# Six of sixteen weight tiles of a modulation gate move from TensorE to VectorE, and their partial sums are added in a later block

## The reference, cut to what matters

```python
def modulate(x, norm_g, ada):
    shift, scale, gate = jnp.split(ada, 3, axis=-1)
    return rmsnorm(x, norm_g) * (1 + scale) + shift, gate

def mixer_layer(x, xc, c_act, cc_act, norm_g, w_ada, b_ada, w_in, ...):
    h, gate = modulate(x, norm_g, (c_act @ w_ada + b_ada)[:, None, :])
    hc, gate_c = modulate(xc, norm_g, cc_act @ w_ada + b_ada)
    u = h @ w_in
    ...                      # convolution, recurrence, windowed attention, each with its own gate path
    x = x + gate * (jnp.concatenate([y_conv, y_lru, y_attn], axis=-1) @ w_out)
    ...
    xc = xc + gate_c * (jnp.concatenate([yc_conv, yc_lru, yc_attn], axis=-1) @ w_out)
```

## Time and profile before

| | us |
|---|---|
| median of 3 runs | 1241.3 |
| lowest, highest | 1240.75, 1241.37 |
| the profiled execution, its time | 1241.5 |
| the profiled execution, span from the first to the last instruction | 1239.7 |
| TensorE busy in the span | 1198.3 |
| VectorE busy | 852.1 |
| ScalarE busy | 555.6 |

### The profile page before, as it was taken

The page is one execution under the profiler, slowest core; times in us unless marked ns, Lnnn a source line. Parts: engine busy times, 40 slices in busy tenths (PEclk is TensorE's granted clock), DMA queues, the critical chain, the costliest instruction groups (busy, mean ns, idle before and its releaser), DMA issues.

```text
span 1239.7 us, 16341 instructions
## 1 busy us (share of the span) xinstructions
PE 1198.3 (97%) x6518; PEld 958.5 (77%) x6518; DVE 852.1 (69%) x1291; ACT 555.6 (45%) x873; POOL 10.2 (1%) x13
## 2 busy tenths in 40 slices
PE   2899999999999999999999999999999999999996
PEld 1556777767778788886888887988978988899885
DVE  5444546767656677663768998695899977657664
ACT  5222446662224434454442222454865455575542
POOL 0000100000000000000000001000000000000000
PEclk9999999999999999999999999999999999999998
DMA  9999856556753442221538887444432634325552
GB/s 335 350 348 348 257 200 250 204 204 241 277 215 133 144 162 84 69 68 68 197 122 350 324 329 261 128 140 135 138 106 77 222 136 149 122 100 202 189 171 68
DMA packets 80892, 236.32 MB, mean 191 GB/s; under 512 B 9392, under 2 KB 54192, under 8 KB 59440
## 3 DMA queue, kind: packets, MB, share of 16 engines
q1 hardware_dynamic: 80816, 235.27, 53.9%
HBM read 230.54 MB, written 2.10 MB: 188 GB/s over the span
## 4 chain that ended last, share of the span: by engine, by line
PE 88%; SPq 4%; DMA 4%; DVE 2%; ACT 2%; issue 0%; DVEq 0%; ACTq 0%
PE psum_block L837 20%; PE psum_block L838 20%; PE psum_block L839 20%; PE psum_block L834 5%; SPq L609 3%; PE psum_ada L663 3%; PE psum_block L835 2%; DMA raw<-in_w_ada 2%; PE psum_scores L919 1%; PE psum_scores L906 1%; PE psum_scores L939 1%; PE psum_scores L869 1%; PE psum_ada L710 1%; DMA bd<-in_w_ada 1%; DMA glu<-in_w_ada 1%; PE psum_misc L966 1%
## 5 line engine op out<-in xcount | busy, mean ns | idle before, releaser
L837 PE MATMUL psum_block<-h_parts,w_hi 128*128 128x512 f32 (+1 forms) x1408 | 494.3, 351 | 0.3 <-DVE h_parts L1413 0.3
L838 PE MATMUL psum_block<-h_parts,w_hi 128*128 128x512 f32 (+1 forms) x1408 | 485.3, 345 | 0.0
L839 PE MATMUL psum_block<-h_parts,w_lo 128*128 128x512 f32 (+1 forms) x1408 | 485.3, 345 | 0.0
L1421 DVE TENSOR_TENSOR w_lo<-raw,w_hi 128x1024 fp32r<-128x1024 f32 x210 | 254.6, 1223 | 257.8 <-ACT w_hi L1061 257.7
L1061 ACT ACTIVATE w_hi<-raw 128x1024 fp32r<-128x1024 f32 x210 | 220.1, 1056 | 413.5 <-PE psum_block L839 354.4
L837 PEld LDWEIGHTS psum_block<-h_parts,w_hi 128*128 128x128 f32 x1408 | 266.6, 189 | 51.5 <-issue 16.8
L838 PEld LDWEIGHTS psum_block<-h_parts,w_hi 128*128 128x128 f32 x1408 | 266.8, 189 | 33.5 <-issue 2.6
L839 PEld LDWEIGHTS psum_block<-h_parts,w_lo 128*128 128x128 f32 x1408 | 266.7, 189 | 32.4
L1706 DVE SCALAR_TENSOR_TENSOR Y<-glu,small,Y 128x512 f32<-128x512 f32 (+1 forms) x240 | 130.4, 612 | 0.0
L834 PE MATMUL psum_block<-h_parts,w_hi 128*128 128x512 f32 x240 | 84.8, 399 | 0.0
L835 PE MATMUL psum_block<-h_parts,w_lo 128*128 128x256 f32 x240 | 67.4, 281 | 0.0
(11 more groups left out here) (228 smaller groups left out, 1349.1 us busy)
## 6 DMA issues: line engine op xcount, KB each, us to landing
raw<-in_w_blocks SPq DMA_DIRECT2D x105, 1024.0 KB, 4.9
raw<-in_w_ada SPq DMA_DIRECT2D x71, 1024.0 KB, 7.0
glu<-in_w_ada SPq DMA_DIRECT2D x10, 1024.0 KB, 9.9
bd<-in_w_ada SPq DMA_DIRECT2D x10, 1024.0 KB, 9.5
qreg<-in_w_blocks SPq DMA_DIRECT2D x8, 896.0 KB, 11.6
kv<-in_w_ada SPq DMA_DIRECT2D x5, 1024.0 KB, 11.9
Y<-in_xT SPq DMA_DIRECT2D x8, 512.0 KB, 7.8
T<-in_xT SPq DMA_DIRECT2D x16, 256.0 KB, 7.0
```

What stands on the lines that cost most here:

```text
L837: mm(ps[:, cols], hi, hh[:, k, t], start=(at == 0), stop=False)
L838: mm(ps[:, cols], hi, hl[:, k, t], start=False, stop=False)
L839: last = mm(ps[:, cols], lo, hh[:, k, t], start=False, stop=(at == DT - 1))
L1421: V.tensor_tensor(wl[:, u % 4, 0:n], raw_of(item)[:, cols], wh[:, u % 4, 0:n].bitcast(F32), ALU.subtract).then_inc(*C.up("lo", u))
```

## The change

A third way is added for layer 0's gate tiles 10 to 15. VectorE multiplies each with the two conditioning vectors and adds it into running sums, `gate0_acc`: four instructions of 1024 columns per tile (two vectors, two halves), tile 10 with a plain multiplication, the others with multiply and add. The running sums lie in rows 8 to 15 of Y (left 256 columns), in rows 2 and 3, and in the second half of `bd`. Tiles 10 to 14 are loaded one after the other into rows 0, 1, 6 and 7 of Y, a single buffer outside the ring; tile 15 goes through the ring. Block 15 ends with two gate tiles on TensorE and the sum, `gate0_sum`, which is `scale_sum` with other operands. Tiles 0 to 9 move to blocks 9, 11, 12, 13 and 15; layer 1's shift tiles to blocks 16 to 23, one block later each. ScalarE waits for the sum before it splits keys and values (block 18) and before it writes attention gate 0 into Y (block 20).

```diff
+GATE0_ON_DVE = {7: [10, 11], 8: [12], 10: [13], 11: [14], 14: [15]}
+GATE0_LOADS = {8: [11], 9: [12], 10: [13], 12: [14], 14: [15]}
+GATE0_IN_Y = (10, 11, 12, 13, 14)
+GATE0_ON_PE = {9: [0, 1], 11: [2, 3], 12: [4, 5], 13: [6, 7], 15: [8, 9]}
+GATE0_SUM = 15
...
-    s += [("w", b) for b in (OPEN[0], OPEN[0] + 1)]
+    s += [("w", b) for b in (OPEN[0], OPEN[0] + 1)] + [("gate0", GATE0_IN_Y[0])]
...
             if l == 0:
-                s += [("ada", *a) for a in plan.get(b, []) if b != SCALE_SUM] + [("gate", k) for k in gates.get(b, [])]
+                s += [("gate0", k) for k in GATE0_LOADS.get(b, [])]
+                s += [("ada", *a) for a in plan.get(b, []) if a[2] != DT - 1 or a[:2] not in SUMMED]
+                s += [("gate", k) for k in gates.get(b, [])]
...
+            if SLOT[i] == Y_SLOT:
+                return Y[:, 0:12, :].rearrange("p (a b) t -> p a b t", b=6)[:, :, 0:2, :]
...
+            def gate0_sum():
+                pe.wait_ge(*C.at("pick_set"))
+                pe.wait_ge(*C.at("gate0_acc", DT - 1, 3))
+                for i in range(2):
+                    for j in range(4):
+                        part = (Y[:, 8 + 2 * j:10 + 2 * j, 0:LAT] if i == 0 else Y[:, 2 + j, :] if j < 2
+                                else bd[:, 1, 4 * (j - 2):4 * (j - 1), :])
+                        last = mm(psA[32 * j:32 * j + 32, :], pick[:, 32 - i:64 - i], part,
+                                  start=False, stop=(i == 1), tile_position=(0, 32 * j))
+                last.then_inc(*C.up("ada_mm", 0, GATE, DT - 1))
...
+                for n, (i, acc, x) in enumerate(parts_of):
+                    c = cstat[:, c_at(k) + i:c_at(k) + i + 1]
+                    if first:
+                        V.tensor_scalar(acc, x, c, None, ALU.mult).then_inc(*C.up("gate0_acc", k, n))
+                    else:
+                        dve.wait_ge(*C.ago("gate0_acc", 3))
+                        stt(acc, x, c, acc, ALU.mult, ALU.add).then_inc(*C.up("gate0_acc", k, n))
...
+                if gb == OPEN[0]:
+                    gate0_acc(GATE0_ON_DVE[b][0])
...
                 if l == 0:
+                    for k in GATE0_ON_DVE.get(b, [])[1 if b == OPEN[0] else 0:]:
+                        gate0_acc(k)
                     for k in SCALE_ON_DVE.get(b, []):
                         scale_acc(k)
```

More of the change, by code:

```diff
@@ L127, in ada_plan @@
     on_dve = sum(len(tiles) for tiles in SCALE_ON_DVE.values())
[L128 to L132, removed]
+    rest = [(1, SHIFT, k) for k in range(DT)] + [(1, SCL, k) for k in range(DT - on_dve)]
+    plan = {b: [(0, GATE, k) for k in tiles] for b, tiles in GATE0_ON_PE.items()}
+    plan[GATE0_SUM] += [(0, GATE, DT - 1)]
+    first = GATE0_SUM + 1 + DT // 2
+    for b in range(GATE0_SUM + 1, GATE1_AT):
+        if rest and (b < first or (b - first) % 2 == 0):
+            plan[b] = [rest.pop(0) for _ in range(2)]
     assert not rest
@@ L1042, in _ @@
                     misc.append(("pw_out", l, CT - 1))
[L1043 to L1046, removed]
+                for a in PLAN.get(b, []) if l == 0 else []:
+                    if a == (0, GATE, DT - 1):
+                        gate0_sum()
+                    elif a == (1, SCL, DT - 1):
+                        scale_sum()
+                    else:
                         ada_mm(*a)
@@ L1455, in gate_acc, with gate0_acc @@
                     stt(acc, w, cstat[:, c_at(k):c_at(k) + 1], acc, ALU.mult, ALU.add).then_inc(*C.up("gate_acc", k))
+            def gate0_acc(k):
+                w = raw_of(("gate0", k))
+                dve.wait_ge(*arrived(("gate0", k)))
+                halves = ([w[:, a, :, :] for a in range(2)] if k in GATE0_IN_Y else
+                          [w[:, a * 2 * TOK:(a + 1) * 2 * TOK].rearrange("p (m t) -> p m t", t=TOK) for a in range(2)])
+                quarters = [x.rearrange("p m (s t) -> p m s t", t=LAT) for x in halves]
+                latent = Y[:, 8:16, 0:LAT].rearrange("p (a m s) t -> p a m s t", a=2, s=2)
+                parts_of = ((0, latent[:, 0, :, :, :], quarters[0]), (0, latent[:, 1, :, :, :], quarters[1]),
+                            (1, Y[:, 2:4, :], halves[0]),
+                            (1, bd[:, 1, :, :].rearrange("p (m n) c -> p m (n c)", m=2), halves[1]))
+                first = k == min(min(tiles) for tiles in GATE0_ON_DVE.values())
+                if first:
+                    dve.wait_ge(*C.at("h_lo", 0, DT - 1, 1))
+                    dve.wait_ge(*used(last_of(BD_SLOT)))
+                for n, (i, acc, x) in enumerate(parts_of):
+                    c = cstat[:, c_at(k) + i:c_at(k) + i + 1]
+                    if first:
+                        V.tensor_scalar(acc, x, c, None, ALU.mult).then_inc(*C.up("gate0_acc", k, n))
+                    else:
+                        dve.wait_ge(*C.ago("gate0_acc", 3))
+                        stt(acc, x, c, acc, ALU.mult, ALU.add).then_inc(*C.up("gate0_acc", k, n))
             def scale_acc(k):
```

18 lines of the change are left out of this document (16 added, 2 removed).

## The result

The changed kernel takes 1244.06 us (median of 13 runs, 1242.19 to 1245.64), the kernel before in the same comparison 1241.41 us (1240.55 to 1241.91): 2.65 us more, a ratio of 1.0021 with a 95% interval of 1.0012 to 1.0029. The profiled execution took 1243.05 us, with a span of 1241.3 us against 1239.7 us. Lines of the code have moved: L663 is now L687, L1421 is L1462, L609 is L633, L1486 is L1550.

A forecast was written before the change was run, and what follows sets the result against it. TensorE was taken to bound the kernel: -3.7 us of work, +3.9 for waits on tiles 6 and 7, +1.9 for tile 9, about +2.0 us in all. Forecast 1243.3 us, range 1238.3 to 1246.0 us.

The forecast's parts named there:

- TensorE's ledger: Six tiles leave TensorE (5.55 us), block 15's sum adds 1.85 us: net -3.7 us if TensorE never waits.
- VectorE's ledger: Tiles 11 to 15 each add four 1024-column instructions on VectorE, 4.8 us a tile, bounds 4.4 to 5.3 us.
- Blocks 7 to 10 covered: Tiles 10 to 12 fit VectorE's idle gaps there; tile 13 in block 10 costs only 0.7 us.
- The new wait of 4.5 us in block 11: VectorE waits 4.5 us for tile 14, whose load stands behind block 14's weights; the tile ends at 230.2 us.
- The waits in block 13: TensorE waits 2.3 us for the load of gate tile 6 and 1.6 us for tile 7.
- Tile 9: In block 15 TensorE waits 1.9 us for this tile's load, which needs tile 15's buffer and lands at 274.9 us.
- Blocks 16 and 23: TensorE's wait for VectorE's gate values, +1.1 us, returns in block 16; block 23 gains a pair of 1.85 us.
- The clock: Rival, chance 0.16: a block 15 wait halves TensorE's clock, costing 1.6 us (1244.9 us); a block 13 fall costs nothing.
- this threshold: TensorE's clock was to fall only after waits of about 2.1 us or more, from one earlier 2.13 us wait.
- The sign named for it: A granted clock below 1.00 in block 16 would show the main forecast wrong.
- The lead survives: Rival, chance 0.20: VectorE's chain does not end last in blocks 13 and 15, TensorE keeps 3.7 us: 1237.6 us.

The follow-up runs named there:

- fillers: The changed kernel with idle matmuls ahead of tiles 6 and 7 in block 13 and tile 9 in block 15: 1244.07 us (11 runs), 1243.59 us once.
- both apart: The changed kernel with tiles 14 and 15 landing in free qreg columns, tile 14's load ahead of block 14's weights: 1237.72 us.
- four tiles only: The kernel before with only the change's part in blocks 7 to 10, four gate tiles on VectorE, twelve on TensorE: 1240.00 us against 1241.75 us.
- the first profile: The changed kernel's profiled execution from its first measurement, nothing else altered: 1243.05 us.
- the change again: The changed kernel measured again unaltered, on the chip of the other experiments: 1244.36 us against 1241.71 us for the kernel before.
- tile 15 apart: The changed kernel with tile 15 landing in free qreg columns instead of the ring, tile 14 left as it was: 1241.82 us.
- the third look: One more single execution of the changed kernel, unaltered: 1244.34 us against 1241.57 us for the kernel before.
- tile 14's load first: The changed kernel with tile 14's load issued ahead of block 14's weights instead of behind them: 1239.28 us against 1241.73 us before the change.

## Why the prediction was right, and where it was not

The forecast was 2.0 us more. The median shows 2.65 us; with the clock held by fillers it is 2.36 us (11 runs) and 2.02 us (one run; that it comes so near is a single execution's chance).

- **TensorE's ledger, -3.7 us: right.** Without the waits the change brings -4.0 us (both apart), and its first part alone -1.75 us of -1.85.
- **VectorE's ledger: right.** 4.79 us for a tile, 4.8 forecast. The four instructions of 1.28 us overlap, as in the earlier trace rows.
- **Blocks 7 to 10 covered: right** (four tiles only).
- **The new wait of 4.5 us in block 11: right.** 4.70 us; the tile ended at 229.80 us (230.2), block 14's second low half at 236.4 us (236.8).
- **The waits in block 13: over-sized.** 1.59 and 1.40 us, where the step said 2.3 and 1.6. TensorE was there when forecast; the loads came 0.8 us sooner, half of it because SP sent them at 236.47 us, not 236.9 (VectorE's old work of block 10 ended at 210.17 us, not 210.7), the rest because they took 7.3 and 9.8 us from the weights' issue, not 7.6 and 10.1. It cost the sum nothing, since block 15 waits for VectorE's chain and not for TensorE's; so the total could not have shown this error.
- **Tile 9: right.** It waits 1.96 us (1.9 forecast) where the clock holds ahead of it. In that execution TensorE and the load both came about 0.5 us sooner after the start than forecast, so the wait fits better than its two ends do. Counted from the start's last transposes, it starts 136.9 to 137.8 us later in the six profiles with this load order (changed kernel and fillers), 137.3 us on average; the forecast's 274.9 us, counted from 137.57 us before, is 137.3 us.
- **Blocks 16 and 23: right.** The wait for VectorE's values is 1.10 us, the added pair 1.85 us.
- **The clock: the cost right, its condition wrong.** The rival priced a fall behind block 15 at 1.6 us (1.68 measured) and said that one in block 13 would cost nothing, which the first profile shows but for the 0.26 us above. But it was to decide from a wait of 2.1 us on, with a chance of 0.16. The clock fell after 1.92 and 1.96 us, and after 1.59 and 1.40 us with 1.07 us of work between them. So the step that failed is this threshold, taken from one row. The sign named for it, a clock below 1.00 in block 16, did not come either: in the change again the fall ended at 278.1 us and block 16 began at 278.71 us. Holding the clock takes 0.3 us of the 0.65 us by which the median lies above the sum; the rest is no more than landing times and the start move from one execution to the next, and is not settled. How often the clock falls can only be estimated, from the mean granted clock that is on record for each execution: 0.9944 for the kernel before (65 executions), 0.9931 for the changed one (24), 0.9945 with both fillers (11). A fall as long as the first profile's takes 0.0014 off the mean (half of 3.4 us in 1241 us), so the changed kernel has about one more fall per execution than the kernel before, and the one with both fillers none on average. How the falls divide between the blocks is open. The Trainium skill (TensorE: Matmul & The Clock Gate, HAM oscillation) says that waits for data between dense stretches can throttle the array; the waits in its example, about 3 to 5 us, are longer than any here, so it does not by itself carry the rival as the prediction has it. The windows agree where the clock stood at 0.50 behind such a wait, while the same waits in block 13 left it at 1.00 in the change again.
- **The lead survives, 1237.6 us:** it failed for the reason that the prediction gave against it, the order of the two loads. With that order changed the kernel measured 1237.72 us, 4.0 us under the kernel before beside it.

## What to carry to other kernels

Work that is moved into an engine's idle time is free only if its data are there when the idle time is: follow each new load back through the queue that issues it, since a load behind another buffer's wait starts when that buffer is free, not when its own is. An engine that bounds a kernel should be fed so that it does not stand still at all, since two waits of 1.5 us can cost 1.6 us more through the clock. Before a gain is given up, try another place for the load: one entry of the load list was worth 5 us here (+2.65 us with it, -2.45 us with it moved).

## What was not expected of the hardware

The same waits gave a fall of the clock in three profiled executions and none in a fourth: 1.59 and 1.40 us (first profile and tile 15 apart, there 1.41 us) and 1.63 and 1.41 us (the third look), then 0.50, against 1.57 and 1.40 us and 1.00 (the change again). With tile 15 apart the fall lasted from 246.1 to 252.9 us and began while TensorE still waited for tile 7, which started at 246.87 us. Waits of 1.33 us (tile 14's load first) and of 1.10 us (block 16) left it at 1.00 in the profiles.

A load of 1 MB was there within 5.2 us when it was issued alone, and after 7.3 to 8.3 us when a block's weights had been issued 0.4 us ahead of it; and the start of the kernel, the same code in all, had its last transposes anywhere from 137.4 to 138.7 us.
